# Queries of a sparse attention layer turned by DMA instead of TensorE, with the maxima of the next head turned ahead of this head's compressed values

## What is computed

```python
s_c = jnp.einsum('btghd,bngd->bghtn', qc, k_cmp) * scale          # compressed: 31 keys
p_c = masked_softmax(s_c, cmp_end[None, :] <= t[:, None])
o_c = jnp.einsum('bghtn,bngd->btghd', p_c, v_cmp)
...
s_s = jnp.einsum('btghd,bgtkd->bghtk', qc, k_g) * scale           # selected
p_s = masked_softmax(s_s, ...)
o_s = jnp.einsum('bghtk,bgtkd->btghd', p_s, v_g)
...
s_w = jnp.einsum('btghd,bkgd->bghtk', qc, kb) * scale             # window
...
return gc[..., 0:1] * o_c + gc[..., 1:2] * o_s + gc[..., 2:3] * o_w
```

## Time and profile before

| | us |
|---|---|
| median of 3 runs | 869.14 (868.8 to 869.91) |
| the profiled execution, its own time | 868.95 |
| its span | 867.2 |
| PE busy in the span | 848.3 (98%) |
| DVE, ACT, POOL busy in the span | 562.8, 502.0, 485.5 |
| PE clock granted | 1.00 of full over the span |

### The profile page before, as it was taken

How to read it: one execution, slowest core, us unless ns; L and a number is a source line. 1 busy time by engine, 2 the same in 40 slices (tenths; PEclk the granted TensorE clock), 3 DMA queues, 4 the chain that set the end, 5 groups by cost and what they waited for, 6 DMA issues and landing times.

```text
span 867.2 us, 16773 instructions
## 1 busy us (share of the span) xinstructions
PE 848.3 (98%) x6041; PEld 709.4 (82%) x6041; DVE 562.8 (65%) x1607; ACT 502.0 (58%) x1151; POOL 485.5 (56%) x627
## 2 busy tenths in 40 slices
PE   6999999999999999999999999999999999999998
PEld 6999998888888888778888888778887677777786
DVE  5899988887878787653111113278689688888521
ACT  6456667887877778652134223434443789898610
POOL 2000407876767686343347424366675699999731
PEclk9999999999999999999999999999999999999999
DMA  6433322111111101122227222222233100100011
GB/s 217 131 98 98 98 79 77 39 52 51 43 28 37 53 14 50 49 97 97 96 93 134 93 92 65 80 97 74 79 97 97 50 3 2 51 3 2 2 49 49
DMA packets 39324, 58.93 MB, mean 68 GB/s; under 512 B 8757, under 2 KB 22346, under 8 KB 39242
## 3 DMA queue, kind: packets, MB, share of 16 engines
q1 hardware_dynamic: 39200, 57.85, 21.4%
q10 hardware_dynamic: 42, 0.01, 0.0%
HBM read 55.63 MB, written 2.10 MB: 67 GB/s over the span
## 4 chain that ended last, share of the span: by engine, by line
PE 85%; DVE 8%; ACT 3%; issue 2%; POOL 1%; DMA 0%; ACTq 0%; DVEq 0%; POOLq 0%
PE bank L97 19%; PE bank L99 18%; PE bank L98 18%; PE bank L1280 4%; DVE w_lo L2180 2%; PE bank L502 2%; PE bank L484 2%; PE bank L1263 2%; PE bank L511 2%; PE bank L503 2%; PE bank L1231 1%; PE bank L1232 1%; PE bank L591 1%; PE bank L592 1%; PE bank L590 1%
## 5 line engine op out<-in xcount | busy, mean ns | idle before, releaser
L2003 POOL TENSOR_TENSOR w_lo<-w_raw,w_hi 128x2048 fp32r<-128x2048 f32 (+1 forms) x26 | 118.4, 4554 | 124.0 <-ACT w_hi L1728 123.9
L97 PE MATMUL bank<-w_hi,h_hi 128*128 128x512 f32 (+3 forms) x472 | 171.4, 363 | 1.7 <-DVE h_lo L2100 1.0
L99 PE MATMUL bank<-w_hi,h_lo 128*128 128x512 f32 (+3 forms) x472 | 166.8, 353 | 0.0
L98 PE MATMUL bank<-w_lo,h_hi 128*128 128x512 f32 (+3 forms) x472 | 166.8, 353 | 0.0
L1728 ACT ACTIVATE w_hi<-w_raw 128x2048 fp32r<-128x2048 f32 (+1 forms) x26 | 49.2, 1893 | 94.0 <-PE bank L99 94.0
L97 PEld LDWEIGHTS bank<-w_hi,h_hi 128*128 128x128 f32 x472 | 88.7, 188 | 15.1 <-issue 3.4
L99 PEld LDWEIGHTS bank<-w_hi,h_lo 128*128 128x128 f32 x472 | 88.7, 188 | 11.5
L98 PEld LDWEIGHTS bank<-w_lo,h_hi 128*128 128x128 f32 x472 | 88.9, 188 | 10.1
L789 POOL TENSOR_TENSOR p<-kvr,p 128x512 f16<-128x512 f32 (+1 forms) x96 | 88.5, 942 | 10.1 <-ACT p L705 9.9
L97 PE MATMUL bank<-w_hi,o_hi 128*128 128x512 f32 x192 | 77.2, 402 | 0.8 <-DVE o_lo L2340 0.8
L99 PE MATMUL bank<-w_hi,o_lo 128*128 128x512 f32 x192 | 75.8, 395 | 0.0
(11 more groups left out here) (367 smaller groups left out, 2440.9 us busy)
## 6 DMA issues: line engine op xcount, KB each, us to landing
w_raw<-in_nsa_w_in SPq DMA_DIRECT2D x10, 1024.0 KB, 5.0
w_raw<-in_mla_w_in SPq DMA_DIRECT2D x8, 1024.0 KB, 5.2
w_raw<-in_mla_w_out SPq DMA_DIRECT2D x8, 1024.0 KB, 5.0
w_raw<-in_nsa_w_in SPq DMA_DIRECT2D x8, 984.0 KB, 5.0
w_raw<-in_nsa_w_out SPq DMA_DIRECT2D x4, 1024.0 KB, 5.1
w_raw<-in_mla_w_uq SPq DMA_DIRECT2D x7, 576.0 KB, 4.2
w_raw<-in_mla_w_ukv SPq DMA_DIRECT2D x15, 256.0 KB, 2.7
w_raw<-in_mla_w_in SPq DMA_DIRECT2D x4, 704.0 KB, 5.7
```

Source lines behind the costliest of these rows:

```text
L97: nc.tensor.matmul(out, a[0], b[0], start=start, stop=False)
L98: nc.tensor.matmul(out, a[0], b[1], start=False, stop=False)
L99: return nc.tensor.matmul(out, a[1], b[0], start=False, stop=stop)
L2003: nc.gpsimd.tensor_tensor(w_lo[g % 2][:, :, 0:width], w_raw[g % 2][:, :, 0:width], w_hi[g % 2][:, :, 0:width].bitcast(F32), ALU.subtract). ...
```

## The change

The queries of a head are no longer transposed on PE. ACT writes the high part and DVE the low part as float16 with the tokens still on partitions (`q16`, two buffers, padded from 96 to 128 columns with zeros), reading the queries from SBUF; SP then starts one DMA transpose for each head (`turn_q`) into `qT` (three buffers), which holds both parts turned. This runs two heads ahead. Heads 0 and 1 are prepared during the input products, where POOL also clears the padding (`clear_pads`).

The compressed scores are made in three products of 32 columns added in PSUM, so DVE reads them once. `compressed_scores(n + 1)` and `turn_max(n + 1)` now stand at the end of pass n, ahead of `compressed_values(n)`. `turn_max(0)` stands ahead of the last three products of the input stage. Banks 3 and 4 swap their roles in the order of score banks.

```diff
+                    qT = [at_slab(f"qT{a}", 114 + 2 * a, [P, 2, SEQ], F16) for a in range(QR)]
...
+                    q16 = [at_slab(f"q16_{a}", 128 + 2 * a, [P, 2, NT, P], F16) for a in range(QS)]
...
-                    score_bank, x_bank = bank[2:5], bank[7]
+                    score_bank, x_bank = [bank[2], bank[4], bank[3]], bank[7]
...
+                    def turn_q(sp, n):
+
+                        if n == 0:
+                            sp.wait_ge(rows_set, 2)
+                        sp.wait_ge(q_lo, n + 1)
+                        if n:
+                            sp.wait_ge(q_landed, 16 * n)
+                        if n >= QR:
+                            sp.wait_ge(s_done, U * (n - QR + 1))
+                        sp.dma_start_transpose(qT[n % QR][:, :, :].rearrange("d s (t c) -> d (s t) c", t=NT),
+                                               q16[n % QS][:, :, :, :].rearrange("p s t d -> p (s t d)")
+                                               ).then_inc(q_landed, 16)
...
                     def sync(sp):
+                        for n in range(QS, H):
+                            turn_q(sp, n)
...
                             for u in range(2):
                                 large_term(n, u, 0, u)
                                 mask(n, u)
-                                if u == 0 and n + 1 < H:
-                                    turn_q(n + 1)
...
-                                dst = x_bank[:, i * 2 * NC:(i + 1) * 2 * NC]
-                                nc.tensor.matmul(dst, qT_hi[a][0:DK, tok], kcT[:, :, n // HPG, :], start=True, stop=False)
-                                last = nc.tensor.matmul(dst[:, 0:NC], qT_lo[a][:, tok], kcT[:, 0, n // HPG, :],
-                                                        start=False, stop=True)
+                                dst = x_bank[:, i * NC:(i + 1) * NC]
+                                nc.tensor.matmul(dst, qT_hi(n)[0:DK, tok], kcT[:, 0, n // HPG, :], start=True, stop=False)
+                                nc.tensor.matmul(dst, qT_hi(n)[0:DK, tok], kcT[:, 1, n // HPG, :], start=False, stop=False)
+                                last = nc.tensor.matmul(dst, qT_lo(n)[:, tok], kcT[:, 0, n // HPG, :], start=False, stop=True)
...
-                                compressed_scores(n)
-                                turn_max(n)
                                 start_scores(n)
+                                if n == 0:
+                                    pe.wait_ge(r1_made, HALF_GATE)
...
                                     values(n - 1, 3, (1,))
+                                pe.wait_ge(ct_ready, n + 1)
+                                if more:
+                                    compressed_scores(n + 1)
+                                    turn_max(n + 1)
                                 compressed_values(n)
...
+                            nc.scalar.activation(q16[n % QS][:, 0, :, 0:DK], q_head(n), ACT.Copy).then_inc(q_hi, 1)
...
+                    def q_low(dve, n):
+
+                        dve.wait_ge(q_hi, n + 1)
+                        at = q16[n % QS]
+                        nc.vector.tensor_tensor(at[:, 1, :, 0:DK], q_head(n), at[:, 0, :, 0:DK],
+                                                ALU.subtract).then_inc(q_lo, 1)
...
+                    def clear_pads():
+                        for a in range(QS):
+                            last = nc.gpsimd.memset(q16[a][:, :, :, DK:P], 0.0)
+                        last.then_inc(rows_set, 1)
...
-                              (NIN - 1, 0, NT - 1): turn_first_q}
...
+                                        if (c, j, t, k) == (NIN - 1, 1, NT - 1, KP - 1):
+                                            first_max()
...
+                        if s == 14:
+                            pool.wait_ge(kt_turned, 2 * G)
+                            clear_pads()
```

More of the change, by code:

```diff
@@ L427, in sparse_attention @@
                     max_bank = lambda n: bank[0] if n else bank[6]
-                    ct_at, cv_at = x_bank[:, 0:P], bank[6][:, 2 * P - NT:2 * P + NT * DV]
-                    q_turned, q_hi, q_lo, rows_set = sem("q_turned1"), sem("q_hi1"), sem("q_lo1"), sem("rows_set1")
+                    ct_at, cv_at = x_bank[:, P:2 * P], bank[6][:, 2 * P - NT:2 * P + NT * DV]
+                    q_hi, q_lo, q_landed, rows_set = (sem(n) for n in ("q_hi1", "q_lo1", "q_landed1", "rows_set1"))
                     f_done, max_done, m_turned, m_in = sem("f_done1"), sem("max_done1"), sem("m_turned1"), sem("m_in1")
@@ L459, in tensor, with first_scores @@
                     def tensor(pe):
[L460 to L464, removed]
+                        def first_scores(n, u):
+                            k = U * n + u
+                            i, branches = tile_of[u]
+                            tok, keys = slice(i * P, (i + 1) * P), (i + 1) * P
+                            if n == 0 and u == 0:
                                 pe.wait_ge(kt_hi, 2 * G + 1)
                                 pe.wait_ge(kt_lo, 2 * G + 1)
[L467 to L478, removed]
                             if u == 0:
-                                pe.wait_ge(q_hi, n + 1)
+                                pe.wait_ge(q_landed, 16 * (n + 1))
                             if k >= 2:
@@ L510, in large_term @@
                             dst = score_bank[(U * n + u) % 3][:, w * left:(w + 1) * left]
-                            nc.tensor.matmul(dst, kT_hi[0:rows, b, g, keys], qT_hi[a][0:rows, j * P:], start=False, stop=False)
+                            nc.tensor.matmul(dst, kT_hi[0:rows, b, g, keys], qT_hi(n)[0:rows, j * P:], start=False, stop=False)
                         def mask(n, u):
@@ L644, in ahead, with first_max @@
                             first_scores(0, u + 1)
+                            if u + 2 == U:
+                                compressed_scores(0)
+                        def first_max():
+                            turn_max(0)
                         def attend():
@@ L917, in vector @@
                         nc.vector.tensor_copy(identr[:, :], ident[:, :])
-                        low(0)
                         for u in range(U):
@@ L936, in vector @@
                                 leave(n - 2, 1)
+                            if n + QS < H:
+                                q_low(dve, n + QS)
                             if more:
-                                low(n + 1)
                                 maximum(n + 1, 0)
@@ L1447, in turn_k_cmp @@
                         nc.tensor.transpose(bank[4][0:DK, 0:P], kcmp[:, :], ident[:, :]).then_inc(kt_turned, 1)
-                    turn_first_q, ahead, attend = sparse_tensor(pe)
+                    ahead, first_max, attend = sparse_tensor(pe)
                     def turn_most():
@@ L1825, in middle @@
                                  13: [lambda: square1(15), lambda: square1(16), kc_high],
-                                 14: [lambda n=n: square1(n) for n in range(17, 21)],
+                                 14: [lambda n=n: q_high(n) for n in range(2)] + [lambda n=n: square1(n) for n in range(17, 21)],
                                  15: [lambda n=n: square1(n) for n in range(21, 25)],
```

68 lines of the change are left out of this document (32 added, 36 removed).

## The result

The changed kernel takes 875.13 us in the median of 4 runs (874.64 to 875.43), the kernel before 869.52 us beside it (868.8 to 870.17). The ratio is 1.0064, with a 95% interval from 1.0047 to 1.0082. The forecast was 876.1 us and slower. The profiled span grew from 867.2 to 873.0 us, so 5.8 us are to be found.

The account below looks back on a forecast made before the run. PE, busy throughout the heads, was taken as bound with two chains through ACT and DVE ending just in time. Terms 6.4 + 0.2 + 0.5 - 1.1 + 0.5 + 0.5 = +7.0 on 869.14 gave 876.1 us, range 871.5 to 881.5.

Parts of the forecast that it names:

- The head: Time between turned maxima of successive heads: 8.90 us against 8.41, +0.49 each, +6.4 us for 13 heads.
- T: Start of the turned maxima on PE in a head; mask 0 was to move from T + 1.33 to T + 1.85.
- Rival 1: At the joints of both chains: slack of at least 0.5 us each, so the gain arrives, 862.7 us; 7%.
- rival 2: At the two joints: only one costs, a head takes 8.4 to 8.5 us, total 869 to 872 us; 9%.
- chain A: ACT's exponentials of piece 0, from mask 0 to piece 3: 1.58 us, no slack; PE then waits some 0.5 us.
- Chain B: DVE's maxima, from coarse products of piece 2 to the turned maxima: 2.88 us, slack 0.03; PE then waits 0.38.
- Head 1 and the last head: Head 1, 8.72 us before, gets +0.2; the last head, without next maximum, keeps 0.52 us ahead of chain A: +0.5.
- Head 0 and the end of the input products: First small term starts sooner, -1.1 us; spared transposes against late DVE and POOL work on weights' low part, +0.5 together.
- POOL and DVE at SBUF: DVE's low part of the queries waits up to 1.1 us a head, POOL loses about 0.45; +0.5 in all.
- Rival 3: POOL becomes the bound: heads 2 to 9 take 9.5 us, or weights' low parts come late; 880 to 884 us; 14%.
- The transfers: DMA transposes of the queries, needed one head later: hidden, nearer to 2.0 us than to 8.2.
- Rival 4: DMA transposes don't fit: from about 8.5 us each they set the head's length, each further us costs 14; 4%.

Follow-up runs that it names:

- e4: Kernel before, with values(n-1, 1) of the previous head moved ahead of scores(n, 3): 866.99 us, ratio 0.9983, 8.33 us a head.
- e5: Changed kernel, with compressed values first again at the pass's end and values(n-1, 1) moved ahead of scores(n, 3): 867.57 us, ratio 0.9977 to the kernel before.
- e14: Changed kernel, with the copy of the turned compressed exponentials moved from DVE to ACT: 874.76 us, ratio 1.0065 to the kernel before, 8.76 us a head.
- e7: Changed kernel, with DVE's low part of the queries computed twice, first into an unread tile: 877.85 us, ratio 1.0104 to the kernel before.
- e9: Changed kernel, compressed values first again, values(n-1, 1) ahead of scores(n, 3), and POOL's four output-weight parts on DVE: 869.06 us, ratio 1.0002 to the kernel before.
- e6: Changed kernel, with each DMA transpose of the queries done twice, the second after the first landed: 875.84 us, ratio 1.0079 to the kernel before.

## Why the prediction was right

**The head.** The forecast was 3.43 + 2.59 + 2.88 = 8.90 us; measured are 3.39 + 2.59 + 2.88 = 8.86. The price of both chains was right to 0.01 us: 1.57 for 1.58, 2.88 for 2.88. What was mis-sized is the move of mask 0: to T + 1.82, where I had 1.85. 13 heads make +5.8 for +6.4. Of the +7.0 in all, +5.8 came: 0.6 is missing here and 0.5 in the term for SBUF. Rival 1 (the gain arrives) and rival 2 (one joint alone) fall with the two waits that stand in each head.

**The idle times** came out at 0.50 and 0.40 by starts, for the forecast 0.5 and 0.38. The records show only 0.35 and 0.25, in sum 0.60 a head, as the windows say (1.20 for two). PE's ends are modelled; they lie late here, and a wait is told 0.15 us too short. The same made show none where e4 found 0.085, and e5's rows none where chain A took 0.15. PE's own work in a head is thus 8.86 - 0.90 = 7.96 us; the 8.08 of the prediction still held the 0.07 to 0.09 that chain A already cost.

**Chain B** was right as a length but too simple as a mechanism. It has three entrances (the coarse products of piece 2, the transpose, the coarse product of piece 4), 0 and 0.21 us of slack for the first two, and about 0.1 for the third by e14.

**Head 1 and the last head.** +0.14 for +0.2 (8.86 for 8.72), and +0.45 for +0.5 (873.0 - 811.32 = 61.68, against 867.2 - 805.97 = 61.23).

**Head 0 and the end of the input products.** I had -1.1 and +0.5; the turned maxima of head 1 came 0.59 us sooner, at 687.29 for 687.88. The sum was right by luck, both terms were not. Rows of the changed kernel's PE, the last low part and the first small term, beside the earlier trace rows:

```profile
666.19 0.50 PE L97 MATMUL bank<-w_hi,h_hi 128*128 128x512 f32 x1 [0.47 <-POOL w_lo L2026]
...
679.30 0.39 PE L510 MATMUL bank<-qT,kT_hi 96*128 96x512 f16 x1
```

The first small term starts 0.54 us sooner, not 1.1: the scores and turned maxima of head 0 had been moved ahead, not removed, and only the wait of 0.46 us for the gates is really gone. POOL's last low part ended at 661.54 + 4.60 = 666.14 for 665.23, 0.9 late where I had feared 1.4; PE waited 0.47 and, less its transposes, was even 0.17 sooner.

**POOL and DVE at SBUF, +0.5.** Measured: nothing. DVE's low part took 0.55 to 1.5 us as forecast (mean 0.97 in heads 1 to 13; 0.55, so no wait, in the last four), and POOL was busy for 0.39 us more in two early heads where 0.9 was forecast. DVE and POOL had idle time for it. e7 and e9 show that the price is real where they have none. Rival 3 was not wrong about the mechanism, only about the kernel.

**The transfers, hidden.** They land in 3.1 us:

```profile
qT<-q SPq DMA_TRANSPOSE x16, 3.1
```

That is nearer to the 2.0 us of the earlier trace rows than to the 8.2, as I had chosen, and e6 shows that 6 us fit too. Rival 4 asked for 8.5.

With the terms as measured: 5.8 + 0.14 + 0.45 - 0.59 = 5.8 us, the growth of the span.

## What to carry to other kernels

An engine that is busy all the time isn't bound by its work alone: look which waits end just as it arrives, and price each from start to start before taking work off it. Work removed from under a chain, or moved from one side of it to the other, becomes idle time; filling the gap with work that is ready (e4, one line) gave more than the whole change. And when one chain is eased, follow it link by link: the next entrance can be 0.1 us behind.

## What the runs showed of the hardware

- A DMA that transposes eight 128x128 blocks of float16 (256 KB) from SBUF to SBUF took 3.1 us from issue to landing in the median of the change's 16, 3.0 at least and 6.5 at most. The Trainium skill ("VectorE: DVE Perf Modes", section "The three transpose paths") gives 1309 ns for one block (of bf16), an estimated 10.5 us for eight one after another. The trace doesn't agree with that for a transfer of eight blocks.
- A DVE step of 384 elements with both operands in SBUF took 0.55 us or up to 1.44 to 1.5 us, by where POOL's instruction stood. POOL lost less: its run of four steps took 3.32 us in e5 without DVE's step beside it and 3.64 with it, its pair of 512 in e9 2.25 and 2.45. In the rows shown the later one waits: in e9 it was POOL beside DVE's step for the weights (1.10 for 0.64 us).
